# A two-block transformer kernel: gate matmuls regrouped, embedding projection moved to the second layer norm, 25 gathered rows in gate building

## What is computed

```python
x = layer_norm(ALPHA * x + y @ w_out, pg, pb)          # end of both layers of the first block
# second block
h = rmsnorm(x, norm_mix); proj = h @ w_in
merged = gate0 * (gqa_attention(...) @ w_up_att) + gate1 * (hgrn2_bidirectional(...) @ w_up_hg)
x = x + merged @ w_out
x = x + peer_ffn(rmsnorm(x, norm_ffn), wq, subkeys, u, v)   # 16384 experts, 8 heads, 16 picks each
g_ple = sigmoid(rmsnorm(x, norm_ple) @ ple_gate)
x = x + g_ple * (p @ ple_proj)                              # p: 512 x 256, ple_proj: 256 x 1024
```

## Time and profile before

| | us |
|---|---|
| median of 3 runs | 2934.59 |
| lowest, highest | 2931.49, 2937.3 |
| profiled execution, time | 2937.61 |
| profiled execution, span | 2935.5 |
| PE busy | 2741.0 (93%) |
| DVE busy | 1786.8 (61%) |
| ACT busy | 766.3 (26%) |
| POOL busy | 776.4 (26%) |

### The profile page before, as it was taken

One profiled execution on the slowest core, in us unless ns is written; L12 is line 12 of the kernel. 1 busy time (PEld: TensorE's weight loads), 2 busy tenths in 40 slices (PEclk: granted clock), 3 DMA queues, 4 the chain that ended last, 5 costly groups with the idle time before them and its releaser, 6 DMA issues.

```text
span 2935.5 us, 28512 instructions
## 1 busy us (share of the span) xinstructions
PE 2741.0 (93%) x9462; PEld 1589.7 (54%) x9462; DVE 1786.8 (61%) x3592; ACT 766.3 (26%) x2036; POOL 776.4 (26%) x601
## 2 busy tenths in 40 slices
PE   9999999999999899998899988989999899989986
PEld 4454454444565354445654676878888744434432
DVE  3997733008762331357752657899777787757876
ACT  1113410102331021345541232211344411101222
POOL 2830010000000000002210255444422255535664
PEclk9999999999999999999999999999999999999988
DMA  5131122211102212110021499899866599999996
GB/s 201 57 115 58 62 96 86 85 58 68 47 29 72 86 62 86 37 53 29 29 94 72 161 379 384 333 329 320 314 200 202 196 369 409 409 412 409 394 390 224
DMA packets 125763, 544.44 MB, mean 185 GB/s; under 512 B 13888, under 2 KB 14272, under 8 KB 117568
## 3 DMA queue, kind: packets, MB, share of 16 engines
q0 software_dynamic: 73728, 268.47, 24.3%
q1 hardware_dynamic: 49472, 258.02, 23.5%
q10 hardware_dynamic: 2432, 16.29, 1.4%
HBM read 538.52 MB, written 4.19 MB: 185 GB/s over the span
## 4 chain that ended last, share of the span: by engine, by line
PE 66%; DMA 12%; DVE 11%; ACT 4%; issue 4%; POOL 3%; DVEq 0%; ACTq 0%; SPq 0%; POOLq 0%
PE ps L629 14%; PE ps L1216 9%; PE ps L748 7%; DMA STREAM<-experts 6%; PE ps L685 6%; PE ps L1188 6%; PE ps L1007 3%; DMA ROW_V<-peer_v,C 3%; PE ps L905 2%; PE ps L1036 2%; DVE X L2535 2%; PE ps L934 2%; PE ps L1113 2%; ACT ONE L1713 2%; PE ps L1101 2%
## 5 line engine op out<-in xcount | busy, mean ns | idle before, releaser
L1188 PE MATMUL ps<-XTD,STREAM 128*128 128x256 f32 x2048 | 458.7, 382 | 26.1 <-ACT GD L1706 17.9
L629 PE MATMUL ps<-XT,W 128*128 128x512 f32 (+1 forms) x1216 | 471.8, 548 | 6.9 <-issue 4.5
L1216 PE MATMUL ps<-STREAM,GD 128*128 128x512 f32 x1024 | 456.0, 602 | 20.4 <-DMA STREAM<-experts 16.8
L1188 PEld LDWEIGHTS ps<-XTD,STREAM 128*128 128x128 f32 x2048 | 386.1, 191 | 84.8 <-issue 18.6
L1874 POOL DMA_INDIRECT ROW_U<-peer_u,C x208 | 262.6, 1262 | 403.0 <-DVE DOT L2523 384.4
L629 PEld LDWEIGHTS ps<-XT,W 128*128 128x128 f32 x1216 | 229.6, 190 | 248.0 <-issue 238.4
L1216 PEld LDWEIGHTS ps<-STREAM,GD 128*128 128x128 f32 x1024 | 190.4, 191 | 284.3 <-issue 202.1
L2535 DVE SCALAR_TENSOR_TENSOR X<-ROW_V,WEIGHT,X 128x1024 f32<-128x1024 f32 x208 | 267.1, 1284 | 93.9 <-DMA ROW_V<-peer_v,C 82.4
L2523 DVE CUSTOM_DVE_ANT_0 ROW_U<-ROW_U,XN 128x1024 f32<-128x1024 f32 x208 | 253.7, 1220 | 58.1 <-DMA ROW_U<-peer_u,C 56.6
L1883 POOL DMA_INDIRECT ROW_V<-peer_v,C x208 | 235.4, 1132 | 158.1 <-DVE X L2535 122.4
L748 PE MATMUL ps<-W,Y 128*128 128x512 f32 x512 | 221.8, 594 | 3.7 <-ACT H L1307 1.4
(11 more groups left out here) (353 smaller groups left out, 3640.3 us busy)
## 6 DMA issues: line engine op xcount, KB each, us to landing
STREAM<-experts SPq DMA_DIRECT2D x256, 512.0 KB, 6.7
W<-wstream SPq DMA_DIRECT2D x53, 2048.0 KB, 8.5
GD<-wstream ACTq DMA_DIRECT2D x2, 2048.0 KB, 15.5
ROW_U<-peer_u,C POOLq DMA_INDIRECT x208, 10.1
ROW_V<-peer_v,C POOLq DMA_INDIRECT x208, 10.1
XT<-xT SPq DMA_DIRECT2D x8, 256.0 KB, 5.4
W<-wstream SPq DMA_DIRECT2D x8, 256.0 KB, 5.6
X<-x SPq DMA_DIRECT2D x1, 2048.0 KB, 18.9
```

The lines of the kernel that those rows point to most:

```text
L629: mm = pe.matmul(b[:, 0:rhs[k].shape[-1]], w[:, k, m * P:(m + 1) * P], rhs[k], start=(k == 0), stop=(k == KD - 1))
L1188: mm = pe.matmul(UP_BANK[g % 2][:, 0:256], u[:, k, :], XTD[:, k, :], start=(k == 0), stop=(k == KD - 1))
L1216: mm = pe.matmul(acc(b, n)[:, :], GD[:, i * 256 + b * P:i * 256 + (b + 1) * P], STREAM[m % STREAM_RING][:, n * T:(n + 1) * T], start=(i == ...
```

## The change

- `gate_matmuls`: four gate matmuls now stand ahead of unit 0 and of every odd unit, two ahead of each other unit (and so ahead of `head_outputs`), and one (two at the first two levels of even units from 2 on) after each level. Still 12 to a unit. ACT's copies of their banks follow by `hgate_level`.
- `p @ ple_proj`: its operands are loaded on ACT's queue before `out_b` is drained, 8 groups of 2 matmuls stand after `out_b` on PE, ACT copies 8 banks to `G` and stores them to DRAM (2 MB). Near the end four loads of 0.5 MB bring them back, in place of 1.5 MB of operands, and `ple_proj` goes from the end. `ple_transposes` no longer waits for `y_ready`; the gate matmuls of calls 1 and 3 wait for `ple_gate_ready` instead.
- Dense queries of blocks 2, 3 are made in the order of heads 2, 3, 0, 1, so that the two weight slots that are still in `W` are used again: two loads of 2 MB less. Routing takes the blocks in the same order.
- ACT's `row_weights` before tile 0: 11, 14, then 17, 22, 27, 32 (before: 14, then 20, 26, 32, 38). `weighed_by(g)` lets ACT stay three tiles behind `rows_by` until tile 60.
- DVE's order of the first rows: routing steps of unit 1 stand between rows, not in one piece; `residual_sum(3)` stands after row 7, not after row 3.
- Exponentials, their normalisation, the turned picks and their copy come 5, 6, 8 and 9 tiles after `PICKED` (before: 2, 3, 5, 6).
- `rows_by` grows by 5 in 9 tiles in gate building, not 1 in 2: 120 rows by tile 127, not 117.
- The kept scores are loaded 8 rows earlier.

```diff
+SOFT_AFTER, SOFT_END, TURNED, TURNED_COPY = 5, 6, 8, 9
+DENSE_HEADS = (2, 3, 0, 1)
...
-    return rows_by(QUAD_FROM) + (g - QUAD_FROM) // 2
+    return rows_by(QUAD_FROM) + (g - QUAD_FROM) * 5 // 9
...
+def weighed_by(g):
+    return 34 + 2 * g if g < 3 else rows_by(g - 3 if g < 60 else g) - LAG
...
+def hgates_first(unit):
+    return 2 if unit % 2 == 0 and unit > 0 else 4
+def hgates_at(unit, l):
+    return 1 + (l < 4 - hgates_first(unit))
...
             out_projection("out_b")
+            pe.wait_ge(loaded_proj, 32)
+            for n in range(8):
+                b, half = n // 2, n % 2
+                if n < 4:
+                    bk = ps[4 + n]
...
+                for k in range(2):
+                    mm = pe.matmul(bk[:, :], PLE_P[:, k, b * P:(b + 1) * P], PROJ[:, k, half * T:(half + 1) * T],
...
+            gate_matmuls(hgates_first(0))
             direction(0, 0)
             for i in range(HG_HEADS - 1):
+                gate_matmuls(hgates_first(2 * i + 1))
                 direction(i, 1)
+                gate_matmuls(hgates_first(2 * i + 2))
                 head_outputs(i)
                 direction(i + 1, 0)
                 outputs_transposed(i)
+            gate_matmuls(hgates_first(2 * HG_HEADS - 1))
             direction(HG_HEADS - 1, 1)
...
-            out_projection("out_b", 6, 2)
...
+            out_projection("out_b", 6, 2, first_embedded)
+            for n in range(2, 8):
+                embedded(n)
+            ac.after(ac.n)
+            act.wait_ge(bank_free, POS["emb"] + 4 + 4)
+            act.dma_start(emb_kept, EMB_OUT).then_inc(emb_stored, 16)
...
             queries("wq3a", 3, (0, 1))
-            row_weights(14)
+            row_weights(11)
             columns_gained(2)
             columns_gained(3)
-            for q in range(4):
-                queries(f"wq{q}b", q, (2, 3))
-                row_weights(20 + 6 * q)
+            row_weights(14)
+            for i, q in enumerate(DENSE_HEADS):
+                queries(f"wq{i}b", q, (2, 3))
+                row_weights(17 + 5 * i)
...
             rows_to(4)
-            while routed < 2:
-                draw_to(drawn + 1)
+            draw_to(ROUTE_STEPS + 13)
+            rows_to(6)
+            draw_to(ROUTE_STEPS + 23)
+            rows_to(8)
             residual_sum(3)
-            rows_to(6)
+            rows_to(9)
             row_factor(3)
-            rows_to(rows_by(-1))
+            for r in range(10, rows_by(-1) + 1):
+                draw_to(min(ROUTE_STEPS + 23 + 2 * (r - 9), 2 * ROUTE_STEPS + 2))
+                rows_to(r)
...
-                    dve.wait_ge(ple_proj_full, 2 * i + n + 1)
-                    ch.link(dve.tensor_tensor(gate, gate, ps[PLE_J[i][n]][:, :], ALU.mult))
+                    if n == 0:
+                        dve.wait_ge(loaded_emb, 48 if i < 3 else 64)
+                    ch.link(dve.tensor_tensor(gate, gate, EMB[i][:, n * T:(n + 1) * T], ALU.mult))
```

More of the change, by code:

```diff
@@ L173, in gqa_pos @@
     return POS["gqa"] + FILL_C.index(what)
+def hgates_first(unit):
+    return 2 if unit % 2 == 0 and unit > 0 else 4
+def hgates_at(unit, l):
+    return 1 + (l < 4 - hgates_first(unit))
 def hgate_level(j):
-    return -(-16 * (j + 1) // 3) - 1
+    made = 0
+    for unit in range(2 * HG_HEADS):
+        made += hgates_first(unit)
+        for l in range(LEVELS + 1):
+            made += hgates_at(unit, l)
+            if made >= KD * (j + 1):
+                return (LEVELS + 1) * unit + l
 def gate_step(stage, j):
@@ L1015, in _, with gate_matmuls @@
             hgates = hgate_fill()
-            def gate_matmuls(unit, l):
-                for _ in range(1 + (l % 2)):
+            def gate_matmuls(n):
+                for _ in range(n):
                     next(hgates)
@@ L1245, in ple_gates @@
                 mm.then_inc(ple_full, 1)
-            def ple_proj(i):
-                b = PLE_ORDER[i]
-                w = PROJ.rearrange("p (k n) -> p k n", k=2)
-                pe.wait_ge(loaded_proj, 32)
-                if i == 3:
-                    pe.wait_ge(ple_gate_ready, 6)
-                for n in range(2):
-                    for k in range(2):
-                        mm = pe.matmul(ps[PLE_J[i][n]][:, :], PLE_P[:, k, b * P:(b + 1) * P], w[:, k, n * T:(n + 1) * T],
-                                       start=(k == 0), stop=(k == 1))
-                    mm.then_inc(ple_proj_full, 1)
             pe.wait_ge(tail_free, made)
@@ L1352, in att_steps, with embedded, out_projection @@
                             (gate_silu if stage == "a" else gate_tanh)(j)
-            def out_projection(name, n, roots=1):
+            def embedded(n):
+                dst = EMB_OUT[:, n * T:(n + 1) * T]
+                if n < 4:
+                    act.wait_ge(emb_full, n + 1)
+                    ac.count(act.activation(dst, ps[4 + n][:, :], ACT.Copy))
+                else:
+                    act.wait_ge(bank_full, POS["emb"] + n - 3)
+                    act.activation(dst, ring(POS["emb"] + n - 4)[:, :], ACT.Copy).then_inc(bank_free, 1)
+            def out_projection(name, n, roots=1, last=None):
                 for half in range(2):
@@ L1359, in out_projection @@
                         if half == 1:
-                            for _ in range(roots):
+                            for r in range(roots):
                                 n += 1
                                 block_root(b, n)
+                                if b == NB - 1 and r == 0 and last is not None:
+                                    last()
             def x_transposes(name):
@@ L1787, in _ @@
                     scale_quad(q)
-                row_weights(rows_by(g) - LAG)
+                row_weights(weighed_by(g))
                 for q in quads_of(g):
```

73 lines of the change are left out of this document (45 added, 28 removed).

## The result

The kernel with the change takes 2905.44 us (median of four runs, 2901.85 to 2909.42), beside 2935.64 us for the kernel before (four runs). The ratio is 0.99, its 95% interval 0.9882 to 0.9917: 30 us faster. The prediction said 2880 us: the sign was right, and of the 55 us forecast 30 came. The profiled execution took 2909.42 us, with a span of 2907.3 us and a mean granted clock of 0.982.

A forecast was written before the change was run, and what follows sets the result against it. It took PE's own work to bound the kernel (66% of the chain of waits). Terms: -30 + 3 - 15 - 7 + 3 - 9 = -55, from the median of 2934.6 to 2880 us; range 2865 to 2906.

The forecast's parts named there:

- Scan: At unit starts and head outputs, gate matmuls fill PE's waits and keep its clock up: 30 us faster, lower bound 15.
- The scan keeps its pace: Rival, chance 0.2: the chain over DVE, ACT and POOL sets 2.2 us a level; scan gives 15, not 30; 2895 us.
- Embeddings at the second layer norm: Products moved behind `out_b` make `aq` start later: 3 us slower, ends 2.4 and 5; store and loads cost nothing.
- Dense queries and first tiles: Three waits of PE, for `XTD`, at the third query and at tile 1, shrink: 15 us faster.
- From these I expect DVE 17 us ahead at row 46: In the gathered rows, two spared loads (10.5 us) and routing between rows (10 us) put DVE 17 us ahead.
- DVE does not get ahead: Rival, chance 0.2: gather latency holds the rows, DVE gains 5 us, queries and picks give 12, not 22; 2890 us.
- DVE sets the pace from the first gathered row to the last quad: Rival, chance 0.03: PE's 22 us are lost, gate building costs 44 us more; 8 us slower, 2943 us.
- Picks: At the picks of blocks 2 and 3, three tiles of delay spare PE's wait: 7 us faster, 0 to 10.
- sign of being wrong: At the picks, ACT still waiting over 5 us would show the forecast wrong.
- Gate building: Three more gathered rows there: 3 us slower, ends 0 and 7.5.
- End: Tile sums and end: three rows fewer, kept scores issued earlier, `ple_proj` gone: 9 us faster, ends 4 and 13.

The follow-up runs named there:

- early-norm kernel: The change, with the normalisation of block 2's picks 0 tiles, not 6, after DVE asks for the exponentials; 2900.25 us.
- woven, early norm: The change, with row weights between query drains, normalisation 0 and 2 tiles after the asking, block 2's exponentials, turned picks and copy at 8, 10, 11 tiles; 2892.75 us.
- scan alone: The kernel before, with only the regrouped gate matmuls of the scan; 2911.18 us, ratio 0.9917.

## Why the prediction was right and where it failed

- **Scan: right.** -28.3 us for a forecast of -30. PE's five waits of 18.8 us for POOL's keys are now seven of 0.6 us at most, and a level takes PE 1.75 us (from 1379.85 to 1381.60 below), as forecast, not 2.2; the granted clock was 1.00 throughout. "The scan keeps its pace" is refuted (its bound of 15 us adds up to 15.7); running alone it gives 24 us of time. PE's timeline in unit 5, where the earlier trace rows had the slow levels:

```profile
1379.85 1.05 PE L1076 MATMUL ps<-H 128*128 128x128 f32 x8
...
1381.60 1.05 PE L1076 MATMUL ps<-H 128*128 128x128 f32 x8
```

- **Embeddings at the second layer norm: right at `aq`, 2.8 us missed behind it.** From the end of `out_b` to the start of `aq` it was 20.6 us and is 22.3, so +1.7 for a forecast of +3. The rest of that stage's +4.7 the prediction had at nothing: 2.8 us lie between `aq` and the last product ahead of the scan (261.6 us from start to start, now 264.4). They stand at the first scores of the next attention. The kernel before, then the changed one:

```profile
1197.61 1.28 ACT L1506 ACT_TABLE_LOAD   x1
```

```profile
1202.35 1.28 ACT L1559 ACT_TABLE_LOAD   x1 [2.94 <-DVE NM L2269]
1205.14 1.93 PE L988 MATMUL ps<-H,Y 64*128 64x512 f32 x4 [1.94 <-ACT QC L1559]
```

  ACT's table load stood in its idle time ahead of the wait for DVE and now stands behind it. PE waits 1.94 us for the exponentials, not 0.7; then the granted clock is 0.50 from 1205.4 to 1208.7 us, where it had stayed at 1.00. In the early-norm kernel the same wait left the clock at 1.00, and there the stretch takes 262.8 us: 1.2 us are the later table load, 1.6 the clock. The one edit of ACT's list there is its wait for the 2 MB store, ahead of these steps; that this moved the load was not tried. The timeline of PE at the second layer norm:

```profile
1019.57 13.99 PE L928 MATMUL ps<-XN,XT 128*128 128x512 f32 x32 [0.38 <-issue]
1033.40 1.91 PE L698 MATMUL ps<-C,H 128*128 128x128 f32 x16
1037.41 3.35 PE L698 MATMUL ps<-C,H 128*128 128x128 f32 x16 [2.10 <-ACT XT L1513]
1041.54 23.87 PE L945 MATMUL ps<-W,XT 128*128 128x512 f32 x55 [0.78 <-ACT XT L1513]
```

  The first half of the turned rows, behind the embedding products, takes 1.91 us; the second, behind a wait of 2.10 us, takes 3.35; and `aq` still starts at full speed: 23.87 / 55 = 0.434 us each, as before. The granted clock was 0.50 from 1038.4 to 1041.3 us and 1.00 from 1041.54, where `aq` starts, so it rose behind nothing but turned rows. The Trainium skill, TensorE: Matmul & The Clock Gate, Part 4, has it that transposes don't count as a busy PE; by it `aq` would have started at half clock and the term been 5. This trace disagrees, as the prediction had taken it.

- **Dense queries and first tiles: right in themselves, worth nothing.** Tile 0 comes 4.9 us earlier against the first routing step, and PE's hole of 9.77 us at tile 1 is gone: 15 of PE's time. The step that failed is the next one: *"From these I expect DVE 17 us ahead at row 46"*. It failed twice.

  First, DVE's sum needs the row and its weight, and the prediction costed only the row: 19.7 us of waiting for weights (and 4.0 more for the product ahead of `residual_sum(3)`) took the place of the 21.8 us that the waits for rows had lost, and ask 2 stood at 339.9 for 341.0. Second, with the weights in time the waits for rows fall by 10.8 us (13.3 in the kernel "woven, early norm"), not 21, and ask 2 comes 9.6 us earlier than before (331.4), not 17: the term was mis-sized as well. Taken away alone, with the weights late, the spared loads and the routing order change the waits for rows by 1 and 2 us.

  The prediction had looked at ACT's pieces as a matter of PE only ("ACT does 3 row weights ahead of it, not 6"), and never asked who waits for the weights that are then not made.

  In its own terms the rival "DVE does not get ahead" came true in its outcome, and harder than priced: it had kept 12 of 22 us for queries and picks. Its reason was the latency of the gathers; what the trace shows is ACT's late weights. The rival "DVE sets the pace from the first gathered row to the last quad", held at 0.03, had the first half right, with PE's 22 us lost; its 44 us in gate building did not come.

  A wait of the kind stood in the rows already: the 7.2 us "issue" of the earlier trace rows, which the prediction read as time that DVE had in hand, are a sum that waits for ACT's weight. DVE's timeline and ACT's, in the kernel before:

```profile
2106.17 1.28 DVE L2535 SCALAR_TENSOR_TENSOR X<-ROW_V,WEIGHT,X 128x1024 f32<-128x1024 f32 x1 [7.24 <-issue]
```

```profile
2105.79 0.29 ACT L1663 ACTIVATE WEIGHT<-ACTED,C 128x1 f32<-128x1 f32 x1
```

- **Picks: wrong in the mechanism.** The three tiles of delay were to give PE 10.5 us of room (I took 7). They gave none, since `soft_end` was moved by three of DVE's tiles as well, and DVE was the one behind. PE's wait grew from 8.14 to 23.88 us, and ACT's for DVE from 11.2 to 16.5, over the 5 us that the prediction had named as the sign of being wrong.

- **Gate building: right in size by luck.** Forecast +3; measured from first one-hot to first sum +0.5, from PE's first quad +3.4, of which 3 us are the lead that DVE lost before. The stage is best counted from DVE's first one-hot: in the twelve kernels with 22 or 25 rows there it is 246.0 to 249.3 us, however early PE comes. The price per row, 0.7 us for three, holds for these few only; at eight more it is 2.45.

- **End: right.** -8.4 for -9, by 4.5 for the rows (the prediction had up to 7.5) and 3.9 for the rest, not taken apart. The kept scores are waited for 0.3 us, not 8.48. The wait for the dense sums is 3.84 us where it was 11.04:

```profile
2817.39 3.67 PE L1275 MATMUL ps<-C,GD 128*128 128x128 f32 x16 [3.84 <-DVE GD L2665]
...
2881.82 1.97 PE L1275 MATMUL ps<-C,X 128*128 128x128 f32 x8 [29.41 <-DVEq L2597]
```

  Behind the gate matmuls of two calls PE then idles for 29.41 us until the last gathered row: the end is DVE's, and the matmuls of `ple_proj` that left it stood in PE's idle time.

What the terms had in common: I read a stage as PE's because PE was busy for 90% of it, and summed PE's waits. The pace from the first routing step to the tile sums is DVE's with what feeds it, and two runs show it from both sides: in scan alone PE's first tile product moved by 3.2 us and none of DVE's marks did, while eight rows less of DVE's own moved the first one-hot by 17.7.

**What stays open.** What routing between the rows is worth once the weights are in time was not tried. Which of the gathers' waits are due to bytes and which to the ring of three tiles was not taken apart. Why gate building charges 0.7 us for each of the first three rows and 2.45 for the next eight is not known; no count between was tried. The variation of some 5 us in the ask, and of 3 us ahead of the scan, between kernels with the same code has no cause shown.

## What to carry to other kernels

Cut the trace at instructions of the engine that you suspect of setting the pace, and then take work from that engine alone and see whether the stretch shrinks by as much; where it does, PE's waits inside it are a symptom and no saving, however busy PE is. Where an in-order list serves two engines, making a piece smaller for one of them makes it late for the other; weave such work between the drains in which the serving engine idles. And a step that is postponed to give an engine room must not be postponed on the engine that is late.

## What was not expected of the hardware

- Sparing 4.2 MB in a stretch where DMA is busy for 0.86 was worth 0 us (2904.82 against 2905.44) while DVE waited 19.7 us for weights, and 7 us (2905.47 against 2898.56) where it waited for none.
- The granted clock went from 0.50 (1038.4 to 1041.3 us) to 1.00 (from 1041.54) over turned rows alone.
- After waits of 13.42 and 10.46 us PE ran 32 tile products in 9.28 us and the next 64 in 16.14, where 64 take 14.08 in an undisturbed stretch, with the clock at 0.50 for the first 4.3 and 5.0 us: the waits cost some 4 us beside themselves.
- After the same wait of 1.94 us the clock was 0.50 for 3.3 us in the change and stayed at 1.00 in the early-norm kernel.
